# Two runs of matmuls for each weight unit: rounded weights first, remainder second

## What is computed

```python
proj = xn @ w_in                                   # 2048 x (3072 + 1024 + ... + 6144)
merged = gate[0] * (y_dn @ w_br_dn) + gate[1] * (y_swa @ w_br_swa) + gate[2] * (y_sb @ w_br_sb)
y = merged @ w_o
q, kv = hn @ w_xq, mem_n @ w_xkv                   # cross attention, then o @ w_xo
up = hn @ w_up                                     # 2048 x 8192, then (silu(gate) * val) @ w_down
u = h @ conv_w_in; y = silu(layer_norm(conv(u))) @ conv_w_out
x = x + g * (relu(h @ mlp_w1) ** 2 @ mlp_w2)       # 2048 x 8192 x 2048
```

## Time and profile before

| | |
|---|---|
| time, median of 3 runs | 2598.98 us (2597.12, 2598.98, 2601.64) |
| profiled execution: span, first to last instruction | 2598.0 us |
| mean granted clock of PE over the span | 0.996 |
| instructions in the span | 38,652 |
| PE matmuls | busy 2546.5 us, 98% |
| PE weight loads (PEld, beside the matmuls) | busy 2183.6 us, 84% |
| DVE, ACT, POOL | busy 1874.6, 1284.9, 232.0 us |
| DMA | 554 MB, mean 213 GB/s |

### The profile page before, as it was taken

One profiled execution on the slowest core, in us unless ns is written; L12 is line 12 of the kernel. 1 busy time (PEld: TensorE's weight loads), 2 busy tenths in 40 slices (PEclk: granted clock), 3 DMA queues, 4 the chain that ended last, 5 costly groups with the idle time before them and its releaser, 6 DMA issues. The chain is left out here.

```text
span 2598.0 us, 38652 instructions
## 1 busy us (share of the span) xinstructions
PE 2546.5 (98%) x14491; PEld 2183.6 (84%) x14491; DVE 1874.6 (72%) x2099; ACT 1284.9 (49%) x1677; POOL 232.0 (9%) x272
## 2 busy tenths in 40 slices
PE   8999999999999999999999999998999999999999
PEld 7888888888887888888888879997788888888887
DVE  6786657868778868887688757988776565565564
ACT  5654545544444547544445556676543344343443
POOL 2000000000000000000000005771000000000000
PEclk9999999999999999999999999999999999999999
DMA  6643446889899765778777745544676656656655
GB/s 207 175 131 106 138 121 228 284 272 333 270 314 314 259 232 176 266 267 280 252 236 265 242 152 161 159 152 166 227 242 224 195 184 191 185 183 199 189 188 168
DMA packets 291667, 554.21 MB, mean 213 GB/s; under 512 B 17153, under 2 KB 96066, under 8 KB 290626
## 3 DMA queue, kind: packets, MB, share of 16 engines
q1 hardware_dynamic: 270994, 442.06, 52.5%
q0 software_dynamic: 18896, 103.83, 12.0%
q10 hardware_dynamic: 1632, 6.29, 0.6%
HBM read 550.01 MB, written 2.11 MB: 213 GB/s over the span
## 5 line engine op out<-in xcount | busy, mean ns | idle before, releaser
L630 DVE TENSOR_TENSOR w_lo<-raw,w_hi 128x1024 fp32r<-128x1024 f32 x814 | 1004.3, 1241 | 620.1 <-ACT w_hi L621 618.8
L621 ACT ACTIVATE w_hi<-raw 128x1024 fp32r<-128x1024 f32 x814 | 859.9, 1060 | 1170.8 <-PE sums L676 435.1
L709 PE MATMUL sums<-x_two,w_hi 128*128 128x512 f32 x1024 | 364.5, 400 | 2.6 <-DVE x_two L1058 1.9
L709 PE MATMUL small<-x_two,w_hi 128*128 128x512 f32 x1024 | 361.2, 398 | 0.0
L711 PE MATMUL sums<-x_two,w_lo 128*128 128x256 f32 x1024 | 287.9, 281 | 0.0
L711 PE MATMUL small<-x_two,w_lo 128*128 128x256 f32 x1024 | 286.8, 280 | 0.0
L676 PE MATMUL sums<-w_hi,x_two 128*128 128x512 f32 x896 | 281.8, 392 | 0.0
L676 PE MATMUL sums<-w_hi,y_hi 128*128 128x512 f32 x672 | 263.8, 393 | 7.2 <-issue 7.2
L676 PE MATMUL sums<-w_lo,y_hi 128*128 128x512 f32 x672 | 262.3, 390 | 0.0
L676 PE MATMUL sums<-w_hi,y_lo 128*128 128x512 f32 x672 | 262.3, 390 | 0.0
L709 PEld LDWEIGHTS sums<-x_two,w_hi 128*128 128x128 f32 x1024 | 193.6, 189 | 50.9 <-issue 3.6
(11 more groups left out here) (446 smaller groups left out, 3887.7 us busy)
## 6 DMA issues: line engine op xcount, KB each, us to landing
raw<-in_mlp_w_dram SPq DMA_DIRECT2D x256, 512.0 KB, 4.1
raw<-in_w_in_dram SPq DMA_DIRECT2D x198, 512.0 KB, 4.1
mod_raw<-in_mod_w_dram POOLq DMA_DIRECT2D x112, 768.0 KB, 6.1
raw<-in_w_up_dram SPq DMA_DIRECT2D x128, 512.0 KB, 3.9
raw<-in_w_down_dram SPq DMA_DIRECT2D x64, 512.0 KB, 4.5
raw<-in_conv_w_in_dram SPq DMA_DIRECT2D x128, 256.0 KB, 3.8
raw<-in_w_o_dram SPq DMA_DIRECT2D x32, 512.0 KB, 6.4
raw<-in_conv_w_out_dram SPq DMA_DIRECT2D x32, 512.0 KB, 4.9
```

Source lines behind the costliest of these rows:

```text
L621: act.activation(w_hi[:, s.slot(k), :], raw[:, s.slot(k), :], ACT.Copy).then_inc(hi_ready, 1)
L630: dve.tensor_tensor(w_lo[:, s.slot(k), :], raw[:, s.slot(k), :], w_hi[:, s.slot(k), :].bitcast(F32), ALU.subtract).then_inc(lo_ready, 1)
L709: pe.matmul(to[:, b, :], w_hi[:, s.slot(k), c], both, start=kt == 0, stop=False, skip_group_check=True)
```

## The change

In `multiply_two` and `multiply_pair` PE waits for `hi_ready`, issues the unit's eight matmuls of 512 columns with w_hi, waits for `lo_ready`, and issues the eight of 256 columns with w_lo. In `multiply` the same is done by a loop over the parts "hi" and "lo" (turned: all (w_hi, a_hi), (w_hi, a_lo), then all (w_lo, a_hi)); in a last unit that is ordered by halves, each half has its hi part and then its lo part. Whole units have one part, as before. The number of matmuls, their operands, the signals and all other engines' programs stay as they were.

```diff
--- before.py
+++ after.py
@@ -652,29 +652,35 @@
                     pe.wait_ge(raw_loaded[s.slot(k)], s.loads(k))
                     halves_loaded(pe, s, k)
                 else:
-                    pe.wait_ge(lo_ready, s.rounds(k + 1))
+                    pe.wait_ge(hi_ready, s.rounds(k + 1))
                 hi = (raw if whole else w_hi)[:, s.slot(k), :].rearrange("p (t n) -> p t n", n=width)
                 lo = w_lo[:, s.slot(k), :].rearrange("p (t n) -> p t n", n=width)
                 order = [(t, b) for t in range(n) for b in range(width // P if turned else TT)]
+                halves = [order]
                 if first_half is not None and k == s.size - 1:
-                    order.sort(key=lambda tb: tb[1])
-                for t, b in order:
-                    kt = k * n + t
-                    end = kt == s.size * n - 1
-                    if turned:
-                        o = sums[:, s.pair, b // 2, (b % 2) * T:(b % 2 + 1) * T]
-                        wh, wl = hi[:, t, b * P:(b + 1) * P], lo[:, t, b * P:(b + 1) * P]
-                        ah, al = a_hi[:, k0 + kt, :], a_lo[:, k0 + kt, :]
-                        first = kt == 0 and b % 2 == 0
-                        steps = [(wh, x_whole[:, kt, 0, :])] if whole else [(wh, ah), (wh, al), (wl, ah)]
-                    else:
-                        o = sums[:, s.pair, b, 0:width] if to is None else to[:, b, 0:width]
-                        ah, al = a_hi[:, k0 + kt, b * P:(b + 1) * P], a_lo[:, k0 + kt, b * P:(b + 1) * P]
-                        first = kt == 0
-                        steps = [(ah, hi[:, t, :]), (ah, lo[:, t, :]), (al, hi[:, t, :])]
-                    for i, (l, r) in enumerate(steps):
-                        mm = pe.matmul(o, l, r, start=first and i == 0, stop=end and i + 1 == len(steps), skip_group_check=True)
-                    if first_half is not None and end and b == 0:
+                    halves = [[(t, b) for t, b in order if b == h] for h in range(TT)]
+                for h, tiles in enumerate(halves):
+                    for part in (("whole",) if whole else ("hi", "lo")):
+                        if part == "lo" and h == 0:
+                            pe.wait_ge(lo_ready, s.rounds(k + 1))
+                        for t, b in tiles:
+                            kt = k * n + t
+                            end = kt == s.size * n - 1
+                            if turned:
+                                o = sums[:, s.pair, b // 2, (b % 2) * T:(b % 2 + 1) * T]
+                                wh, wl = hi[:, t, b * P:(b + 1) * P], lo[:, t, b * P:(b + 1) * P]
+                                ah, al = a_hi[:, k0 + kt, :], a_lo[:, k0 + kt, :]
+                                first = kt == 0 and b % 2 == 0
+                                steps = {"whole": [(wh, x_whole[:, kt, 0, :])], "hi": [(wh, ah), (wh, al)], "lo": [(wl, ah)]}[part]
+                            else:
+                                o = sums[:, s.pair, b, 0:width] if to is None else to[:, b, 0:width]
+                                ah, al = a_hi[:, k0 + kt, b * P:(b + 1) * P], a_lo[:, k0 + kt, b * P:(b + 1) * P]
+                                first = kt == 0
+                                steps = {"hi": [(ah, hi[:, t, :]), (al, hi[:, t, :])], "lo": [(ah, lo[:, t, :])]}[part]
+                            for i, (l, r) in enumerate(steps):
+                                mm = pe.matmul(o, l, r, start=first and i == 0 and part != "lo",
+                                               stop=end and part != "hi" and i + 1 == len(steps), skip_group_check=True)
+                    if first_half is not None and k == s.size - 1 and h == 0:
                         mm.then_inc(first_half, 1)
                 mm.then_inc(unit_used, 1)
                 if beside is not None:
@@ -708,6 +714,10 @@
                     c = slice(t * CH + b * P, t * CH + (b + 1) * P)
                     pe.matmul(to[:, b, :], w_hi[:, s.slot(k), c], both, start=kt == 0, stop=False,
                               skip_group_check=True)
+                pe.wait_ge(lo_ready, s.rounds(k + 1))
+                for t, b in order:
+                    kt = k * UK + t
+                    c = slice(t * CH + b * P, t * CH + (b + 1) * P)
                     mm = pe.matmul(to[:, b, 0:T], w_lo[:, s.slot(k), c], x_two[:, kt, 0, :], start=False,
                                    stop=kt == KT - 1, skip_group_check=True)
                 mm.then_inc(unit_used, 1)
@@ -727,6 +737,11 @@
                         c = slice((2 * t + b) * P, (2 * t + b + 1) * P)
                         pe.matmul(sums[:, s.pair, b, :], w_hi[:, s.slot(k), c], both, start=kt == 0, stop=False,
                                   skip_group_check=True)
+                pe.wait_ge(lo_ready, s.rounds(k + 1))
+                for t in range(n):
+                    kt = k * n + t
+                    for b in range(2):
+                        c = slice((2 * t + b) * P, (2 * t + b + 1) * P)
                         mm = pe.matmul(sums[:, s.pair, b, 0:T], w_lo[:, s.slot(k), c], x_two[:, kt, 0, :], start=False,
                                        stop=kt == KT - 1, skip_group_check=True)
                 mm.then_inc(unit_used, 1)
```

## The result

The changed kernel takes 2584.78 us (median of 4 runs, 2583.95 to 2587.07) against 2599.48 us of the kernel before beside it (2597.12 to 2601.64). The ratio is 0.9943, with a 95% interval of 0.9931 to 0.9956. The prediction was 2585 us. In a second measurement, beside other kernels before it, the same kernel gave 2585.96 us, ratio 0.9948 (0.9934 to 0.9961). The execution of after that was profiled took 2587.07 us, the longest of its four, with a span of 2585.2 us. So a time lies some 1.9 us above the span of the same execution, and before's profile, with its span of 2598.0 us, is that of an execution of about 2599.9 us, which is not under the median of 2598.98.

A forecast was written before the change was run, and what follows sets the result against it. PE was taken as the bound, busy 2546.5 of 2598.0 us, through its matmul spacing. The terms, -11.4 - 3.5 + 0.8 = -14.1 us, took the median of 2598.98 to 2585 us; 8-in-10 range 2574 to 2603.

The forecast's parts named there:

- Grouping: In multiply_two and multiply_pair, runs of one width replace alternating widths on PE; 11.4 us gained, bounds 0 and 17.7.
- The early wait: PE starts a unit once the rounded weights are ready; 3.5 of 5.2 us of stalls on w_lo gained.
- The mid-unit wait: The remainder's wait, now inside about 810 units, is met when PE arrives; 1 ns each, 0.8 us lost.
- A: PE's two rates don't come from alternating widths, so only the stalls are gained; about 2596 us; chance 0.20.
- B: 512-column runs of x_two go at mix_out's slow 0.2344 us a matmul; 2604 to 2624 us; chance 0.10.
- C: The wait inside each unit breaks PE's stream; up to 85 us lost, about 2670; chance 0.05.
- D: More gained: free width changes, most multiply_pair units slow today, mix_out back at 0.2267; 25 us, about 2574; chance 0.07.
- The loss or gain by chance: Around 1770 and 1875 us the granted clock drops after stalls; a stall that shifts there moves 2 to 4 us.
- Units of 2.77 to 2.78 us: Sign in the MLP: eight 512-column matmuls 0.2267 us apart, then eight of 256 columns 0.120 apart.
- First FFN half no quicker: Sign at 1000 to 1130 us, where pairs already ran at the quick rate: units no quicker than before.
- Later units 0.05 quicker: Sign in the later FFN half: each unit 0.05 us quicker than before.
- Less than 2 us on w_lo: Sign in PE's waits: stalls on the weights' remainder under 2 us in total, without new ones in mid-unit.

The follow-up runs named there:

- the met wait: The kernel before with one more wait, for hi_ready and always met by then, in mid-unit in all three routines; 2599.00 us, ratio 0.9999.
- grouping alone: The changed kernel's order with one wait for the remainder ahead of each unit, as in the kernel before; 2596.46 us, ratio 0.9986.

## Why the prediction came true, step by step

That the time was hit to 0.2 us is luck in good part. The mechanism was right, but the terms of the sum, put right by the traces, give -7.4 - 5.0 = -12.4 us and not -14.1. The medians lie 14.7 us apart (13.5 at an equal clock of 0.997), and the 2 us between 12.4 and that have no term: they are of the size by which two executions of the same kernel differ. The base was misread as well. The span of 2598.0 was compared with a median of times, which lie some 1.9 us above their spans; this changes nothing, as the sum was taken from the median.

*Grouping, -11.4 us: right in mechanism, too large.* It is 7.4 us by the traces. Two terms were mis-sized. The change of width in both directions was charged the 6.7 ns of a pair and costs 19 ns at runs of eight, so a unit falls from 2.827 to 2.793, 0.034 and not 0.047. And the quick units were counted as unchanged. They were at 2.773 and rose to 2.793, 0.02 each over some 52 units, 1 us. I had read the excess of a pair as the price of a change and carried it to longer runs. The trace of before had no run of x_two against w_hi from which to see that it grows. That the quick rate would end by grouping had no term in the sum. multiply, priced at 0 for its order, stayed so: the L681 streams keep 0.2267.

*The early wait, -3.5 us: too small.* It is 5.0 us by the stalls in the trace, nearly the whole of the 5.2 that before showed. I had expected x_two and pad to be late next at the two stalls of the start. They were not: the one of 1.5 us gave 1.26 or 1.27 in all eight traces whose multiply starts early, and what is late next there is w_hi, by 0.4. The one of 1.0 us went whole. By the medians at equal clock it is 6.5 to 8.4 us, with one execution on one side at two of the three clocks.

*The mid-unit wait, +0.8 us: nothing.* Three readings say so: the met wait's ratio of 0.9999, equal MLP chunks with one wait and with two, and no pause in the step from hi to lo. The Trainium skill (Advanced Engine Details and Errata, Miscellaneous Facts, Network/Comms) gives 50 to 100 ns for a semaphore's reading; none of it stands in PE's stream here, with 3 ns as the upper bound.

*Rivals.* A, the two rates belong to something else, was half right: one code has two prices, and it changes from one to the other at breaks, as its clause on a phase after a pause said. But grouping took the usual price away wherever it stood. B fell: the 512-column run takes 1.84 us for eight, 0.230 each with its change of width, under the 0.2334 from which B decides. C fell by the met wait. D fell by the joints. The loss or gain by chance came as said, by the clock, 1.16 and 1.36 us in two MLP stages, and also by waits of 0.8, 1.5 and 0.5 us that I had not named.

*What would show it.* Units of 2.77 to 2.78 us: 2.793, missed by 0.015. First FFN half no quicker: so. Later units 0.05 quicker: 0.033. No pause from hi to lo: so. Less than 2 us on w_lo: none. L681 streams at 0.2267: so.

The Trainium skill (TensorE: Matmul & The Clock Gate, Back-to-back issue gap) gives, at 2.4 GHz, the columns over 2.4 plus 2.5 ns as the gap of an isolated matmul, 216 ns for 512 columns, and about 131 ns in a stream with weight loads. This case's uniform stream has 226.7 ns with granted clock 1.00, above both. By its formula, in which only the columns count, all the orders above would take the same time a unit; they lie between 2.773 and 2.827 us, and the measurement decides.

## What to carry to other kernels

Where PE is never idle, its time lies in the spacing of its matmuls; read it as the distance of starts over a long stretch, for each order of widths that the kernel has. Runs of eight matmuls of one moving width are worth 1.2% over the usual rate of alternating ones (2.793 against 2.827 us a unit) and lose 0.7% to their quick rate (2.773). A wait that is met costs nothing that could be measured in the middle of them, so put each operand's wait ahead of its own run. Make a sum from the prices of the order that you build, not from those of the old one: the price of a change of width is not the same in another pattern.

## What the runs showed of the hardware that was not expected

- The excess for one pair of width changes grows with the run length, 3.4, 16, 19 and 18 ns at 2, 4, 8 and 16 matmuls, and at length 1 it is 6.7 or 0. The cause is open. The order of banks is excluded (5.59 us for two units either way), and so is the second write to one bank (2.820 a unit when shifted).
- One stream of alternating widths has two prices, 0.3533 and 0.3467 us a pair, at granted clock 1.00. It changes from one to the other only where it is broken: in before at a stall of 0.65 us, at two small matmuls, and at twelve, with 130 us of the quick rate between the last two; in the kernel with one grouped unit also at that unit. With the pairs shifted by one step the price is 0.3525 behind the two small matmuls and behind the twelve alike. A met wait in mid-stream breaks nothing. What in a break picks the rate was not found.
- A stretch of 25 us with a wait of 1.8 us in it has a granted clock of 0.93 in some executions and of 1.00 in others, with the same instructions (after, first and second execution). The mean clocks 0.995 and 0.997 lie 2.6 us apart in before (2601.2 and 2598.6). That is a part of why grouping alone shows 2.9 us in its medians and 7.3 in its profile: at equal clock it shows 5.0 to 6.0. Why its clock is lower more often than after's, and where the rest of the difference comes from, stays open. So kernels that differ by 0.1 to 0.2% are compared at equal mean clock, or by the unit times in their traces.
